# Decode rows of the token-major projections: fp32 on four column groups of TensorE instead of a fifth tile of split products

## The chip, the cores and the metric

The kernel runs on one NeuronCore of a Trainium2 chip. The metric is the device time of one execution in microseconds; the median of several runs is compared. The profile is one execution taken by the hardware profiler. Engines are called PE (TensorE, the matrix engine), DVE (VectorE), ACT (ScalarE), POOL (GpSimd) and SP (SyncE, which issues the DMAs).

## The reference

One inference step of a decoder of two layers, for two groups of requests that share all weights: a prompt of 512 tokens, and eight sequences that decode one token each. Each layer normalises and modulates its input, projects it, runs three token mixers side by side (retention, differential attention, RWKV-7), merges them by gates, and ends with a squared-ReLU MLP. What the change touches is one line of it, for the columns of retention and of differential attention:

```
h = rms_norm(x, p['norm1'][l]) * (1 + sc1) + sh1
z = jnp.einsum('bld,de->ble', h, p['w_in'][l])
z_ret, z_diff, z_rwkv, z_gate = jnp.split(z, [...], axis=-1)
```

`h` has 1024 columns, `z_ret` 2048 and `z_diff` 1536. All is float32, for 512 + 8 tokens.

## The kernel before

Activations lie with the model dimension on the partitions: `hT` is 8 tiles (k) of 128 rows by T = 520 tokens, of which the last 8 are the decode tokens. A product in fp32 is made of three in the type fp32r: both operands are split in a high and a low part, and high x high, low x high and high x low are added up in PSUM. ACT makes the high part of a weight block (`split_hi`, L546), DVE the low part (`split_lo`, L554), each for half a block (four of the eight k tiles, 128x2048) at a time, into the two pairs of buffers `w_split`. PE's matrix products are all issued from L379 (`mm`) and its transposes from L382.

`token_major` (L803) makes the projections whose result has tokens on the partitions. It is called twice in each layer: for retention with four blocks of 512 columns (L921), and for differential attention with three (L1128). A block `b` has two halves `n = 2b` and `2b + 1` (`u` is 0 or 1), one for each half of the contraction. For each half PE goes over five tiles of tokens m: four of 128 prompt tokens, and a fifth that starts at token 512, has the 8 decode tokens in its first rows, and takes the next 120 columns of `h_raw` along. Each tile has one PSUM bank, `pb[m]`, and each half of it is 4 k tiles x 3 products of 128x128 (activations, held in the array) by 128x512 (weights, streamed):

```
for x, (h, w) in enumerate(((0, wh), (1, wh), (0, wl))):
    t = mm(pb[m], h_raw[h][:, tk], w[:, k, :], start=(u == 0 and k == 0 and x == 0),
           stop=(u == 1 and k == 3 and x == 2))
```

Behind the second half of a tile ACT copies the bank into `arena` (L872): 128x512, and 8x512 for the fifth. The order on ACT within a block is: wait for the end of the first half (`split_free`), split the first half of the next block, five evictions, split the second half of the next block.

The weights come by SP's `load_w` (L531) into two ring slots of 2 MB, block b into slot b % 2; the first two are loaded ahead, the loads of blocks 2 and 3 wait until DVE has split the last half of the block that holds the slot (`slot_free`). In the retention stage SP then issues the first loads of gate weights (`gate_load`, L746). At this stage's start (`before`) DVE and ACT make the activation tiles one by one (`h_ready` counts them) while PE already runs the first half, k by k.

Where PE multiplies nine conditioning rows by a weight block (`ada_rows`, L1191, and `rows` in `start_pe`), the kernel has a form of its own: fp32 without a split, the operand held in the array is 128x32, the k tiles go to four groups of 32 columns of the array in turn (output partitions 0, 32, 64 and 96), and a product with the constant `fold` adds the four partial sums.

All stages are separated by block barriers. The semaphores of the table `sems` are cleared one by one on POOL (`clear`, L372) before the layers and at the end of each.

Of the kernel before, what the change touches and what calls it, by code (L numbers as in the profile page):

```python
# [23 lines left out]
P = 128  # L24
D = 1024
KD = D // P
# [178 lines left out]
def build(nc, a, consts, outs):  # L205
# [7 lines left out]
    with ExitStack() as ctx:  # L213
# [29 lines left out]
        rstd = sb("rstd", T)[:, :]  # L243
        small = sb("small", 512)[:, :]
        pages = sb("pages", DEC * NPG, I32, 1)[:, :]
        AR = 18688
        arena_at = aligned(nc.sbuf_base)
        arena = sb("arena", AR)[:, :]
# [50 lines left out]
        def sem(name):  # L299
# [1 line left out]


        sems = {n: sem(n) for n in (
            "split_high", "split_ready", "split_free", "y_split", "slot0_full", "slot1_full", "slot2_full", "slot3_full", "slot0_free", "slot1_free", "slot2_free", "slot3_free", "loaded", "states_loaded", "stored",
            "pe_for_dve", "dve_for_pe", "pe_for_act", "act_for_pe", "dve_for_act", "act_for_dve",
            "dve_done", "act_done", "dve_for_sp", *(f"page{n}_full" for n in range(10)), "page_free",
            "scores_ready", "scores_read", "logits_ready", "exp_ready", "weights_ready", "turned", "turned_read",
# [33 lines left out]
        up_made, up_read, kk_scaled, kk_factor, kk_spread = sems["up_made"], sems["up_read"], sems["kk_scaled"], sems["kk_factor"], sems["kk_spread"]  # L341
        split_high, split_ready, split_free = sems["split_high"], sems["split_ready"], sems["split_free"]
        y_split_ready = sems["y_split"]
        loaded, stored = sems["loaded"], sems["stored"]
        states_loaded = sems["states_loaded"]
        dve_for_sp = sems["dve_for_sp"]
# [79 lines left out]
        with nc.Block() as block:  # L426
# [57 lines left out]
            @block.vector  # L484
            def _(v):
                dv = c["dve"]
                dv(V.memset(tab[NB:NB + 1, :], MASKED))
                dv(V.memset(small, 0.0))
                dv(V.memset(eps, EPS))
                dv(V.memset(eps_ln, LNX_EPS))  # L490
                for h in h_raw:
                    dv(V.memset(h.bitcast(F32)[:, KD * T:], 0.0))
                for k in range(KD):
                    v.wait_ge(pe_for_dve, c["dve_from_pe"].next())
                    V.tensor_copy(xT[:, k, 0:SEQ], pb[k % 4])
                    dv(V.tensor_copy(xT[:, k, SEQ:T], pb[4 + k % 4][:, 0:DEC]))
                    V.sem_inc(dve_for_pe, 1)
                v.wait_ge(act_for_dve, c["dve_from_act"].next())
                dv(V.tensor_tensor(c_gate, c_gate, c_rows, mult))
                V.sem_inc(dve_for_pe, 1)  # L500
                v.wait_ge(pe_for_dve, c["dve_from_pe"].next())
                dv(V.tensor_copy(csT.rearrange("p k s -> p (k s)"), pb[0][:, 0:72]))
                V.sem_inc(dve_for_pe, 1)
                v.wait_ge(pe_for_dve, c["dve_from_pe"].next())
                for h in range(HB):
                    V.tensor_copy(biases[:, h, 0:512], pb[h])
                    V.tensor_copy(biases[:, h, 512:640], pb[4 + h][:, 0:128])
                dv(V.tensor_copy(biasD.rearrange("p g h -> p (g h)"), pb[4][:, 256:256 + NPG * HB]))
                V.sem_inc(dve_for_sp, 1)
# [3 lines left out]
        with nc.Fori(0, DEPTH) as l:  # L513
# [164 lines left out]
            def start_v(v):  # L678
# [49 lines left out]
                for k in range(KD + 1):  # L728
                    if k < KD:
                        V.tensor_scalar(ht[:, k, 0:SEQ], ht[:, k, 0:SEQ], coef[:, k, 0:1],  # L730
                                        modT[:, k, 0:1], mult, add).then_inc(dve_for_act, 1)
                    if k:
                        v.wait_ge(act_for_dve, c["dve_from_act"].next())
                        V.tensor_tensor(hT[1][:, k - 1], ht[:, k - 1], hT[0][:, k - 1].bitcast(F32), sub).then_inc(h_ready, 1)
                dv(V.tensor_tensor(lam, small[:, 6:7], small[:, 7:8], sub))
                dv(V.tensor_tensor(lam, lam, li[:, bass.ds(l, 1), 0:1].rearrange("p a b -> p (a b)"), add))
                dv(V.tensor_scalar(BR("subln"), BR("subln"), li[:, bass.ds(l, 1), 1:2].rearrange("p a b -> p (a b)"), None, mult))
# [62 lines left out]

            upper = ((4, 5), (6, 7))

            def token_major(col0, n_blocks, n_split, gates=False, before=None):  # L803


                with nc.Block() as block:
                    @block.sync
                    def _(sp):
                        if before:
                            before[0](sp)  # L810
                        for b in range(2, n_blocks):
                            load_w(sp, b % 2, w_in[:, col0 + 512 * b:col0 + 512 * (b + 1)])
                        if before:
                            sp.wait_ge(h_ready, KD)
                        if gates:
                            for j in range(4):
                                gate_load(sp, j)

                    @block.tensor
                    def _(pe):  # L820
                        if before:
                            before[1](pe)
                        def product(u, m, k):
                            tk = slice((4 * u + k) * T + m * P, (4 * u + k) * T + (m + 1) * P)
                            wh, wl = (w_split[u][x].rearrange("p (k n) -> p k n", k=4) for x in range(2))
# [3 lines that stand above are left out]
                            return t  # L829

                        for n in range(2 * n_blocks):
                            u = n % 2
                            pe.wait_ge(split_ready, c["split_ready"].next())
                            if before and n == 0:

                                pe.wait_ge(act_for_pe, c["pe_from_act"].next(5))
                                for k in range(5):
                                    pe.wait_ge(h_ready, k + 1)
                                    for m in range(4 if k < 4 else 0):
                                        product(0, m, k)  # L840
                                    if k:
                                        t = product(0, 4, k - 1)
                            for m in (() if before and n == 0 else range(5)):
                                if u == 0:
                                    pe.wait_ge(act_for_pe, c["pe_from_act"].next())
                                for k in range(4):
                                    if before and n == 1 and m == 0:
                                        pe.wait_ge(h_ready, 5 + k)
                                    t = product(u, m, k)
                                if u:  # L850
                                    t.then_inc(pe_for_act, 1)
                            if u == 0:
                                t.then_inc(split_free, 1)
                        c["pe_from_act"].skip(5)

                    @block.scalar
                    def _(s):
                        S.sem_inc(act_for_pe, 5)
                        if before:
                            before[2](s)  # L860
                        if n_split == 0:
                            split_hi(s, w_split, 0, 0, 0)
                        split_hi(s, w_split, 1, 0, 1, first=False)
                        for b in range(n_blocks):

                            s.wait_ge(split_free, c["split_free"].next())
                            if b + 1 < n_blocks:
                                split_hi(s, w_split, 2 * b + 2, (b + 1) % 2, 0)
                            for m in range(5):
                                r = P if m < MT else DEC  # L870
                                s.wait_ge(pe_for_act, c["act_from_pe"].next())
                                c["act"](S.activation(arena[0:r, (b * 5 + m) * 512:(b * 5 + m + 1) * 512],  # L872
                                                      pb[m][0:r, :], ACT.Copy))
                                S.sem_inc(act_for_pe, 1)
                            if b + 1 < n_blocks:
                                split_hi(s, w_split, 2 * b + 3, (b + 1) % 2, 1, first=False)
                        if gates:
                            gate_hi(s, 0)
                            gate_hi(s, 1)
# [38 lines left out]
                return pe_part, dve_part  # L918


            token_major(RET0, 4, 1, gates=True, before=(start_sp, start_pe, start_s, start_v))  # L921
            Z = lambda b: at(arena, b * 2560, 5, 512)
            rot = [at(arena, 10240, 5, 512), at(arena, 12800, 5, 512)]
            qkT = at(arena, 0, 8, T)
# [200 lines left out]
                    pe_part(pe)  # L1125


            token_major(DIFF0, 3, 0)  # L1128
            w_ada_rest = L("w_ada")[:, 4 * 512:12 * 512]
            NA = 6  # L1130
            zq, zk, zv = Z(0), Z(1), Z(2)
# [1566 lines left out]
```

## Time and profile before

| | us |
|---|---|
| median of three runs | 3099.26 |
| lowest, highest | 3096.32, 3105.85 |
| span of the profiled execution | 3092.7 |
| PE busy in it | 2704.7 |
| DVE busy | 1464.7 |
| ACT busy | 820.6 |

The span runs from the first to the last instruction of the profiled execution; the runs' times hold also what lies around it. A line of the views in order of time has the start and the length in us, the engine, the line of the kernel, the operation, what it writes and reads with shapes, how many instructions are merged, and in brackets the idle time of the engine just before and what ended it. PE's records overlap: the distance of their starts tells the rate. One fp32 product leaves two records, one in fp32r leaves one.

### The profile page before, as it was taken

To read this page: it belongs to the slowest core of one execution; us is meant where nothing else is said; L and a number is where in the kernel's file an instruction comes from. 1 tells how busy PE (TensorE), PEld (TensorE's weight loads), DVE (VectorE), ACT (ScalarE), POOL (GpSimd) and SP (SyncE) were. 2 spreads that over 40 slices of the span, in tenths; PEclk is the share of its full clock that TensorE was granted. 3 is DMA by queue.
4 is the path that set the end of the run, shared out by engine and by line. 5 is a ranking of instruction groups with operands and counts; after the bars stand their busy time and mean duration, and the time that the engine had idled before them with its cause. 6 is when DMAs were issued, how large, how long until landed. Compare 5 with 4: busy or idle time off the path is not lost. (4 is left out here: it accounts for less than half of the span.)

```text
span 3092.7 us, 53427 instructions
## 1 busy us (share of the span) xinstructions
PE 2704.7 (87%) x22862; PEld 2389.3 (77%) x22862; DVE 1464.7 (47%) x2073; ACT 820.6 (27%) x1218; POOL 162.0 (5%) x102
## 2 busy tenths in 40 slices
PE   5988888997698898999969879888967979799997
PEld 3777775886588698999958768567946859799997
DVE  3344346434655665334351541744366566633443
ACT  1221214223311323333222111332241114333331
POOL 0011110300000000000000210112000000000000
PEclk9997999996599799999979879999956989899999
DMA  6222345721000341222341330656010015322232
GB/s 257 98 59 58 113 134 185 228 72 52 14 3 3 126 177 66 98 82 83 137 148 35 86 120 23 219 183 200 16 52 15 3 44 178 110 83 82 83 110 109
DMA packets 216310, 305.16 MB, mean 99 GB/s; under 512 B 28021, under 2 KB 97191, under 8 KB 214786
## 3 DMA queue, kind: packets, MB, share of 16 engines
q1 hardware_dynamic: 216066, 301.67, 29.0%
q8 instruction: 182, 2.98, 0.4%
q14 instruction: 62, 0.51, 0.1%
HBM read 266.49 MB, written 35.14 MB: 98 GB/s over the span
## 5 line engine op out<-in xcount | busy, mean ns | idle before, releaser
L379 PE MATMUL pb<-h_high,f_high 128*128 128x260 f32 x1984 | 401.5, 284 | 4.9 <-DVEq L2619 4.9
L379 PE MATMUL pb<-h_low,f_high 128*128 128x260 f32 x1984 | 398.6, 282 | 0.0
L379 PE MATMUL pb<-h_high,f_low 128*128 128x260 f32 x1920 | 387.7, 283 | 0.0
L554 DVE TENSOR_TENSOR w_low<-ring,w_high 128x2048 fp32r<-128x2048 f32 x66 | 151.3, 2293 | 405.7 <-ACT w_high L546 404.3
L379 PEld LDWEIGHTS pb<-h_high,f_high 128*128 128x128 f32 x1984 | 306.5, 188 | 5.3 <-issue 5.3
L379 PEld LDWEIGHTS pb<-h_low,f_high 128*128 128x128 f32 x1984 | 307.6, 189 | 0.0
L554 DVE TENSOR_TENSOR f_low<-ring,f_high 128x2048 fp32r<-128x2048 f32 x60 | 137.6, 2293 | 339.1 <-ACT h_high L548 214.2
L379 PEld LDWEIGHTS pb<-h_high,f_low 128*128 128x128 f32 x1920 | 294.5, 188 | 0.0
L757 POOL TENSOR_TENSOR g_low<-yT,g_high 128x512 fp32r<-128x512 f32 x96 | 159.9, 1670 | 1978.0 <-ACT g_high L753 1978.0
L379 PE MATMUL pb<-w_high,h_high 128*128 128x512 f32 x560 | 224.9, 402 | 20.9 <-DVEq L558 11.7
L379 PE MATMUL pb<-w_low,h_high 128*128 128x512 f32 x560 | 224.2, 400 | 0.0
L379 PE MATMUL pb<-w_high,h_low 128*128 128x512 f32 x560 | 224.0, 400 | 0.0
L546 ACT ACTIVATE w_high<-ring 128x2048 fp32r<-128x2048 f32 x66 | 126.2, 1917 | 333.2 <-PE pb L379 213.9
L546 ACT ACTIVATE f_high<-ring 128x2048 fp32r<-128x2048 f32 x62 | 118.8, 1916 | 352.9 <-PE pb L379 328.0
L379 PE MATMUL pb<-arena 64*64 64x64 f32 (+4 forms) x2320 | 188.4, 299 | 24.5 <-DVE arena L965 9.4
L379 PE MATMUL pb<-h_high,g_high 128*128 128x260 f32 x768 | 166.5, 300 | 42.9 <-POOL g_low L757 22.4
L379 PE MATMUL pb<-h_high,w_high 128*128 128x260 f32 x800 | 167.4, 292 | 31.7 <-DVE h_low L2513 17.1
L379 PEld LDWEIGHTS pb<-arena 64*64 64x64 f32 (+4 forms) x2320 | 141.6, 166 | 60.6 <-issue 40.5
L379 PEld LDWEIGHTS pb<-h_high,g_high 128*128 128x128 f32 x768 | 125.0, 199 | 60.6 <-POOL g_low L757 38.8
L379 PE MATMUL pb<-h_high,w_low 128*128 128x260 f32 x800 | 165.8, 290 | 0.0
L379 PE MATMUL pb<-h_low,w_high 128*128 128x260 f32 x800 | 165.2, 289 | 0.0
L379 PE MATMUL pb<-h_low,g_high 128*128 128x260 f32 x768 | 160.1, 291 | 0.0
(362 smaller groups left out, 4620.2 us busy)
## 6 DMA issues: line engine op xcount, KB each, us to landing
ring<-in_w_ff_dram SPq DMA_DIRECT2D x32, 2048.0 KB, 7.8
ring<-in_w_in_dram SPq DMA_DIRECT2D x20, 2048.0 KB, 9.1
ring<-in_w_ada_dram SPq DMA_DIRECT2D x18, 2048.0 KB, 8.1
yT<-in_w_in_dram SPq DMA_DIRECT2D x96, 256.0 KB, 3.6
arena<-in_w_ada_dram SPq DMA_DIRECT2D x9, 2048.0 KB
gate_spill_dram<-yT SPq DMA_DIRECT2D x48, 260.0 KB, 4.0
arena<-gate_spill_dram SPq DMA_DIRECT2D x12, 1040.0 KB, 5.4
arena<-in_cache_k_diff_dram SPq DMA_DIRECT2D x32, 256.0 KB, 3.1
```

The costliest lines, as they stand in the source:

```text
L379: return PE.matmul(out, lhsT, rhs, start=start, stop=stop, skip_group_check=True)
L546: t = S.activation(ws[n % 2][0], ring[slot][:, u * 2048:(u + 1) * 2048], ACT.Copy)
L554: t = V.tensor_tensor(ws[n % 2][1], ring[slot][:, u * 2048:(u + 1) * 2048], ws[n % 2][0].bitcast(F32), sub)
L757: G.tensor_tensor(g_split[j % 2][1], g_raw[j % 2], g_split[j % 2][0].bitcast(F32), sub).then_inc(gate_ready, 1)
```

## The change

The decode rows leave the five-tile scheme; the four prompt tiles stay. The eight columns of the activations are copied unsplit into a tile of their own, `dec_h` (8 k tiles of 32 columns, 24 of them zero), once a layer. Between the two halves of a block PE makes eight fp32 products, `dec_h[:, k]` (128x32) by the unsplit weights of the ring slot (128x512), k tile k on column group k % 4, into bank 4. ACT copies the bank to `dec_sum`; ahead of the third tile of the second half PE folds the four partial sums by one fp32 product with `fold` into bank 5, and ACT copies 8x512 of it to where the fifth tile's rows were put. Five semaphores are new. SP's loads into a ring slot wait also for the eight products that read it (`dec_made`). The scratch that is reserved for descriptors of dynamic DMAs is cut to 1024 bytes of a partition, which makes the room.

```diff
+        dec_h = sb("dec_h", KD * 32)[:, :].rearrange("p (k n) -> p k n", k=KD)
+        dec_sum = sb("dec_sum", 512)[:, :]
...
+                dv(V.memset(dec_h, 0.0))
...
+                    if k == 4:
+                        V.tensor_copy(dec_h[:, :, 0:DEC], ht[:, :, SEQ:T]).then_inc(dec_ready, 1)
...
                         for b in range(2, n_blocks):
+                            sp.wait_ge(dec_made, first_block + b - 1)
                             load_w(sp, b % 2, w_in[:, col0 + 512 * b:col0 + 512 * (b + 1)])
...
-                                pe.wait_ge(act_for_pe, c["pe_from_act"].next(5))
-                                for k in range(5):
+                                pe.wait_ge(act_for_pe, c["pe_from_act"].next(MT))
+                                for k in range(4):
                                     pe.wait_ge(h_ready, k + 1)
-                                    for m in range(4 if k < 4 else 0):
-                                        product(0, m, k)
-                                    if k:
-                                        t = product(0, 4, k - 1)
-                            for m in (() if before and n == 0 else range(5)):
+                                    for m in range(MT):
+                                        t = product(0, m, k)
+                            for m in (() if before and n == 0 else range(MT)):
                                 if u == 0:
                                     pe.wait_ge(act_for_pe, c["pe_from_act"].next())
+                                if u and m == 2:
+                                    pe.wait_ge(dec_copied, b + 1)
+                                    if b:
+                                        pe.wait_ge(dec_stored, b)
+                                    mm(pb[5][0:DEC, :], C("fold")[:, 0:DEC], dec_sum).then_inc(dec_folded, 1)
...
                             if u == 0:
                                 t.then_inc(split_free, 1)
-                        c["pe_from_act"].skip(5)
+                                pe.wait_ge(dec_ready, 1)
+                                if b:
+                                    pe.wait_ge(dec_copied, b)
+                                w = wslot(n // 2 % 2)
+                                for k in range(KD):
+                                    t = mm(pb[4][32 * (k % 4):32 * (k % 4) + 32, :], dec_h[:, k, :], w[:, k, :],
+                                           start=(k < 4), stop=(k >= 4))
+                                t.then_inc(dec_made, 1)
+                        c["pe_from_act"].skip(MT)
...
                                 split_hi(s, w_split, 2 * b + 2, (b + 1) % 2, 0)
-                            for m in range(5):
-                                r = P if m < MT else DEC
+                            s.wait_ge(dec_made, first_block + b + 1)
+                            if first_block + b:
+                                s.wait_ge(dec_folded, first_block + b)
+                            S.activation(dec_sum, pb[4], ACT.Copy).then_inc(dec_copied, 1)
+                            for m in range(MT):
+                                if m == 2:
+                                    s.wait_ge(dec_folded, first_block + b + 1)
+                                    S.activation(arena[0:DEC, (b * 5 + MT) * 512:(b * 5 + MT + 1) * 512], pb[5][0:DEC, :],
+                                                 ACT.Copy).then_inc(dec_stored, 1)
                                 s.wait_ge(pe_for_act, c["act_from_pe"].next())
...
+                        s.wait_ge(dec_stored, first_block + n_blocks)
...
-    nc = _bacc.Bacc("TRN2", target_bir_lowering=False, num_devices=1)
+    nc = _bacc.Bacc("TRN2", target_bir_lowering=False, num_devices=1, dynamic_dma_scratch_size=1024)
```

In the diff `b` on PE counts the blocks of both calls in a layer, since `first_block` is 0 for the first and 4 for the second.

## Rows read from the trace of the kernel before

**Rows 1.** Page, part 1: busy us (share of the span) xinstructions.

```profile
PE 2704.7 (87%) x22862; PEld 2389.3 (77%) x22862; DVE 1464.7 (47%) x2073; ACT 820.6 (27%) x1218; POOL 162.0 (5%) x102
```

**Rows 2.** Busy times by stretch: us from:to, length, engines, granted clock, DMA.

```profile
core 0: us, PE busy (x) PEld busy (x) DVE busy (x) ACT busy (x) POOL busy (x), PEclk, DMA share, GB/s
83.40:197.40 114.00, 114.00 (x480) 91.56 (x480) 23.53 (x23) 28.51 (x32) 0.00 (x0) 0.98 0.14 46
341.00:422.60 81.60, 81.58 (x351) 65.55 (x349) 9.17 (x4) 16.04 (x18) 0.00 (x0) 1.00 0.07 26
```

**Rows 3.** ACT in order of time, layer 0, retention: start us, us, instruction, idle.

```profile
127.61 1.92 ACT L546 ACTIVATE w_high<-ring 128x2048 fp32r<-128x2048 f32 x1 [11.43 <-PE pb L379]
...
130.40 0.60 ACT L872 ACTIVATE arena<-pb 128x512 f32<-128x512 f32 x1 [0.87 <-PE pb L379]
...
138.77 0.60 ACT L872 ACTIVATE arena<-pb 128x512 f32<-128x512 f32 x1 [2.20 <-PE pb L379]
...
141.55 0.59 ACT L872 ACTIVATE arena<-pb 8x512 f32<-8x512 f32 x1 [2.18 <-PE pb L379]
...
158.28 0.60 ACT L872 ACTIVATE arena<-pb 128x512 f32<-128x512 f32 x1 [0.87 <-PE pb L379]
```

**Rows 4.** PE in order of time, the same stage.

```profile
85.25 0.63 PE L379 MATMUL pb<-w_high,h_low 128*128 128x512 f32 x1
85.68 0.63 PE L379 MATMUL pb<-w_low,h_high 128*128 128x512 f32 x1
...
196.79 0.39 PE L379 MATMUL pb<-w_high,h_low 128*128 128x512 f32 x1
197.02 0.40 PE L379 MATMUL pb<-w_low,h_high 128*128 128x512 f32 x1
```

**Rows 5.** PE in order of time, differential attention, where `ada_rows` runs.

```profile
472.25 0.39 PE L379 MATMUL pb<-arena 128*128 128x128 f32 x2
472.57 1.93 PE L379 MATMUL pb<-ring,arena 128*32 128x512 f32 x16
474.42 0.49 PE L379 MATMUL pb<-arena 64*128 64x128 f32 x4
...
485.90 0.39 PE L379 MATMUL pb<-arena 128*128 128x128 f32 x2
486.12 0.96 PE L379 MATMUL pb<-cst,xT 128*128 128x9 f32 x8
```

**Rows 6.** Busy times by stretch, same stage; columns as in Rows 2.

```profile
482.70:484.60 1.90, 1.90 (x19) 0.45 (x18) 1.76 (x6) 0.28 (x1) 0.00 (x0) 1.00 0.00 0
487.00:490.00 3.00, 0.53 (x6) 0.34 (x5) 2.79 (x8) 1.62 (x5) 0.00 (x0) 1.00 1.03 398
491.30:494.40 3.10, 3.10 (x19) 0.62 (x18) 1.29 (x3) 0.28 (x1) 0.00 (x0) 0.59 0.18 65
```

**Rows 7.** PE in order of time, decode attention.

```profile
527.90 1.12 PE L379 MATMUL pb<-xT,cst 8*128 8x512 f32 x2 [1.15 <-DVEq L1384]
528.95 1.92 PE L379 MATMUL pb<-ring,arena 128*32 128x512 f32 x16
```

**Rows 8.** DVE, then PE in order of time, end of the last layer.

```profile
3070.30 0.17 DVE L2406 TENSOR_TENSOR xT<-xT,small 128x8 f32<-128x8 f32 x1
...
3079.88 1.53 PE L382 MATMUL pb<-cst,xT 128*128 128x128 f32 x6 [11.04 <-PEq L372]
```

**Rows 9.** DVE in order of time: set-up, and start of layer 0's retention stage.

```profile
15.79 0.69 DVE L495 COPY xT<-pb 128x512 f32<-128x512 f32 x1 [13.51 <-PE pb L382]
...
80.79 0.22 DVE L724 TENSOR_TENSOR yT<-yT,coef 128x64 f32<-128x64 f32 x1
```

**Rows 10.** SP's DMA issues in order of time, layer 0's retention stage.

```profile
76.66 42.57 SPq L531 DMA_DIRECT2D ring<-in_w_in_dram  x3
```

**Rows 11.** Page, part 6: weight loads, KB each, median us to landing.

```profile
ring<-in_w_in_dram SPq DMA_DIRECT2D x20, 2048.0 KB, 9.1
```

**Rows 12.** PE's first work behind layer 0's retention stage.

```profile
202.33 0.77 PE L379 MATMUL pb<-h_high,g_high 128*128 128x260 f32 x2 [4.91 <-PEq L806]
```

More of the change, by code:

```diff
@@ L303, in build @@
         sems = {n: sem(n) for n in (
-            "split_high", "split_ready", "split_free", "y_split", "slot0_full", "slot1_full", "slot2_full", "slot3_full", "slot0_free", "slot1_free", "slot2_free", "slot3_free", "loaded", "states_loaded", "stored",
+            "split_high", "split_ready", "split_free", "dec_ready", "dec_made", "dec_copied", "dec_folded", "dec_stored", "y_split", "slot0_full", "slot1_full", "slot2_full", "slot3_full", "slot0_free", "slot1_free", "slot2_free", "slot3_free", "loaded", "states_loaded", "stored",
             "pe_for_dve", "dve_for_pe", "pe_for_act", "act_for_pe", "dve_for_act", "act_for_dve",
@@ L343, in build @@
         y_split_ready = sems["y_split"]
+        dec_ready, dec_made, dec_copied = sems["dec_ready"], sems["dec_made"], sems["dec_copied"]
+        dec_folded, dec_stored = sems["dec_folded"], sems["dec_stored"]
         loaded, stored = sems["loaded"], sems["stored"]
@@ L801, in build, with token_major @@
             upper = ((4, 5), (6, 7))
-            def token_major(col0, n_blocks, n_split, gates=False, before=None):
+            def token_major(col0, n_blocks, n_split, first_block, gates=False, before=None):
                 with nc.Block() as block:
@@ L831, in _ @@
                         for n in range(2 * n_blocks):
-                            u = n % 2
+                            b, u = first_block + n // 2, n % 2
                             pe.wait_ge(split_ready, c["split_ready"].next())
                             if before and n == 0:
-                                pe.wait_ge(act_for_pe, c["pe_from_act"].next(5))
-                                for k in range(5):
+                                pe.wait_ge(act_for_pe, c["pe_from_act"].next(MT))
+                                for k in range(4):
                                     pe.wait_ge(h_ready, k + 1)
-                                    for m in range(4 if k < 4 else 0):
-                                        product(0, m, k)
-                                    if k:
-                                        t = product(0, 4, k - 1)
-                            for m in (() if before and n == 0 else range(5)):
+                                    for m in range(MT):
+                                        t = product(0, m, k)
+                            for m in (() if before and n == 0 else range(MT)):
                                 if u == 0:
                                     pe.wait_ge(act_for_pe, c["pe_from_act"].next())
+                                if u and m == 2:
[3 more added lines that the diff above has]
+                                    mm(pb[5][0:DEC, :], C("fold")[:, 0:DEC], dec_sum).then_inc(dec_folded, 1)
                                 for k in range(4):
@@ L853, in _ @@
                                 t.then_inc(split_free, 1)
-                        c["pe_from_act"].skip(5)
+                                pe.wait_ge(dec_ready, 1)
[7 more added lines that the diff above has]
+                        c["pe_from_act"].skip(MT)
                     @block.scalar
                     def _(s):
-                        S.sem_inc(act_for_pe, 5)
+                        S.sem_inc(act_for_pe, MT)
                         if before:
@@ L868, in _ @@
                                 split_hi(s, w_split, 2 * b + 2, (b + 1) % 2, 0)
-                            for m in range(5):
-                                r = P if m < MT else DEC
+                            s.wait_ge(dec_made, first_block + b + 1)
[7 more added lines that the diff above has]
+                                                 ACT.Copy).then_inc(dec_stored, 1)
                                 s.wait_ge(pe_for_act, c["act_from_pe"].next())
-                                c["act"](S.activation(arena[0:r, (b * 5 + m) * 512:(b * 5 + m + 1) * 512],
-                                                      pb[m][0:r, :], ACT.Copy))
+                                c["act"](S.activation(arena[:, (b * 5 + m) * 512:(b * 5 + m + 1) * 512], pb[m], ACT.Copy))
                                 S.sem_inc(act_for_pe, 1)
@@ L918, in heads_to_columns @@
                 return pe_part, dve_part
-            token_major(RET0, 4, 1, gates=True, before=(start_sp, start_pe, start_s, start_v))
+            token_major(RET0, 4, 1, 0, gates=True, before=(start_sp, start_pe, start_s, start_v))
             Z = lambda b: at(arena, b * 2560, 5, 512)
@@ L1125, in _ @@
                     pe_part(pe)
-            token_major(DIFF0, 3, 0)
+            token_major(DIFF0, 3, 0, 4)
             w_ada_rest = L("w_ada")[:, 4 * 512:12 * 512]
```

## The prediction

> **What bounds the kernel now.** I read the page's busy times first: PE works 87% of the span [rows 1], but that is an average over stages, and the change touches one kind of stage only, `token_major`. So the next view is the busy time of each engine in the stretches in which it runs: layer 0's retention stage (four blocks of 512 columns) from 83.4 to 197.4 us, its differential stage (three blocks) from 341.0 to 422.6, and the same two in layer 1, which read alike. PE is busy 114.00 of 114.00 us and 81.58 of 81.60; DVE has 23.53 and 9.17, ACT 28.51 and 16.04 [rows 2]. Nothing but PE can set the length. Then ACT's own order of time in one block: each eviction starts 2.79 us after the one before (138.77, 141.55), 0.60 long, with 2.18 to 2.20 us of idle that PE ends; the first evictions of two blocks stand 27.88 us apart (130.40, 158.28) [rows 3]. The eviction of 8x512 at 141.55 is the fifth, the decode tile: it holds 8 rows and waits as long as the others, because PE pushes 512 columns through for each product whatever the number of rows that count. Last, PE product by product: starts are 0.23 us apart (196.79, 197.02) and a record lasts 0.39 to 0.40; just after the stage's first start they are 0.43 apart (85.25, 85.68) [rows 4]. The granted clock of the four stretches is 0.98 to 1.00 [rows 2], so nearly all of it runs at 2.4 GHz, and the 0.43 belongs to the first 4 us of the stage, at 1.2 GHz.
>
> **The change, part by part.**
>
> Removed: in each block the fifth tile's 24 products, 12 in each half. By the evictions a tile's 12 take 2.79 us [rows 3], so 24 take 5.58 us of PE, all of it on the path. The fifth eviction (0.6 us of ACT) goes too, and is off the path except at the stage's end, where the fourth tile's eviction, as long, takes its place.
>
> Added on PE, first term: eight fp32 products of 128x32 by 128x512 on four column groups. The trace holds this very form, with the ring as moving operand, where `ada_rows` builds its modulation rows: 16 records (two per product) start at 472.57 and the next product starts at 474.42, 1.85 us later [rows 5]; the granted clock from 482.7 to 484.6, where another such group runs, is 1.00 [rows 6], and the three groups of that kind that I read at that clock agree within 0.01 us. Eight products one after another would be sixteen passes of 0.43 = 6.9 us, so the four groups do run side by side. I take 1.86.
>
> Second term: the fold, one fp32 product of 128x8 by 128x512. The nearest row is 8x128 by 8x512: two records at 527.90, the next product at 528.95, so 1.05 us [rows 7]. I take 1.05; it includes the passage to 32-column products behind it.
>
> Third term: the passage from the full-width stream into each of these two. A full-width product of 128 columns starts at 472.25 and the first 32-column one 0.32 later; the same product ahead of a full-width one takes 0.22 (485.90, 486.12) [rows 5]. So 0.10 for each passage, 0.20 in all.
>
> Sum for a block: 1.86 + 1.05 + 0.20 = 3.11 against 5.58, a gain of 2.47 us. There are 14 blocks (4 + 3 in each of two layers): 34.6 us.
>
> The Trainium skill speaks against the change here: TensorEngine Tiling (Array Packing), section Key Properties, says that a change of tiling mode drains TensorE. If each of four changes in a block cost what a record outlasts its spacing, 0.17 us, an estimate, the gain would be about 2.3 us a block and 33 in all; the rows at 472.25 show a passage of 0.10, so I keep the sum.
>
> Bounds of the unknown: at the least, four rounds of 0.43 (1.72) and two passes for the fold (0.86) with no passage at all: 2.58, gain 3.00, 42.0 in all. At the most, the longest record of such a group (1.92) and of the 527.90 product (1.12), and four passages of 0.40 - 0.23 = 0.17 each [rows 4]: 3.72, gain 1.86, 26.0 in all. I take the middle term by term because its rows are of the same form and clock.
>
> Semaphores: five more are cleared on POOL, by `clear`, three times (ahead of the layers and behind each). The end of the last layer shows the price: DVE's last addition ends at 3070.47, PE's next work starts at 3079.88 [rows 8], and between them lie the clears of the 117 semaphores in the table `sems`: at most 9.41/117 = 0.08 us each, 5 x 3 x 0.08 = 1.2 us, nothing hides it. Taken: 1.2; bounds 0 and 1.2.
>
> At nothing, with their cover: (a) DVE's copy of the eight columns into `dec_h`, 128x64, 0.22 us by its like at 80.79 [rows 9]. It stands in DVE's queue ahead of the fifth to eighth activation tile and the weight split behind them; PE wants these only when it has done 48 products, some 5 us later; without that cover it costs 0.22 a layer. (b) The clearing of `dec_h` at the start: DVE idles 13.51 us there until PE's first transposes [rows 9]. (c) ACT's copy of the partial sums, 0.6 us: ACT has just done the next block's split (1.92 us, 127.61 [rows 3]), the eight products end about when the split does, so the copy is done 3 us after the half ends; PE wants it only before the third tile of the second half, 1.86 + 5.58 = 7.4 us after the half ends. Queued behind ACT's wait for these products are the evictions of the block, the first of which PE allows 4.7 us after the half; so some 2 us are spare. (d) PE's waits for `dec_copied` and `dec_stored` of the block before are met some 20 us ahead. (e) SP's new wait for `dec_made` holds the loads of blocks 2 and 3 and, behind them, the first four gate loads, until the block two before has had its eight products. Now the loads go out from 76.66 on, the last of three by 119.23 [rows 10]. The load of block 2 would leave at about 98 instead of 94, lands in 9.1 us (median) [rows 11], and is wanted when the first half of block 1 is done, 23 us after it leaves. The gate loads move from 120 to about 126 and are wanted at the stage's end, now near 188.
>
> What follows the stage: PE starts the next one 4.91 us idle [rows 12], behind the last eviction, two gate splits and the block's barrier; all of this hangs on the stage's end and moves up with it, and none of it waits for a time of its own.
>
> **Sum.** 34.6 - 1.2 = 33.4 us. The profiled execution's span is 3092.7; the three runs have a median of 3099.26 and a lowest of 3096.32, so some 4 to 7 us lie around the span. Span 3092.7 - 33.4 = 3059.3; median 3099.3 - 33.4 = 3065.9 us.
>
> **The rivals.**
>
> The column groups run one after another in this place (slower). Then the eight products are 6.9 us instead of 1.86, a block costs 8.1 against 5.58, and 14 blocks lose 35 us and 1.2: 3136. It decides from 4.3 us for the eight products on (5.58 less fold and passages). Against it: the same form at 1.85 and 1.86 us [rows 5]; for it only that there the neighbours are short products, and here a saturated stream.
>
> The clock falls (no change, or slower). From 487.0 to 490.0 PE was busy 0.53 of 3.0 us, and the next group of 32-column products ran at a granted clock of 0.59 [rows 6]. If the 32-column products of this change were followed by 4 us at 1.2 GHz, as at the start of the stage, each fall would lose half of these, about 2 us: 14 falls take 28 back and leave 3094; a fall for the fold too would give 3122. Against it: here no idle lies in front, and from 482.7 to 484.6, in a stretch of busy PE, such products ran at 1.00.
>
> The change doesn't free what it says, because something else ends the block. ACT's work in a block is 3.84 of splits and 3.6 of evictions, with one copy more 7.4 against 25 us; DVE's 4.6. Late weights: a load would have to take over 23 us instead of 9.1 before PE waits. Then the gain would shrink towards nothing, 3090 to 3100. I give it little.
>
> The gain is given back in part behind the stages, where later stages meet DMAs or clock falls in another phase: some 10 us of scatter, 3078 to 3090.
>
> **How the numbers follow.** Forecast (gain 25 to 42): 0.83. Given back in part, still over 0.3%: 0.07. Clock falls once a block, or late weights, within 0.3%: 0.05. Groups in series or two clock falls, slower: 0.05. A measurement of this kernel tells about 0.3%, 9.3 us, from no change: faster is below 3090, slower above 3108.6. Faster 0.90, same 0.05, slower 0.05. Range: from the largest gain, 42.0 with no price for the clears, 3057, to the smallest, 26.0 - 1.2, 3074.5; the runs of the kernel before spread some 3 us below and 6 above their median, so 3055 to 3079.
>
> **What would show each step.** The first evictions of neighbouring blocks stand 25.4 us apart instead of 27.9; the retention stretch is 104 us instead of 114, the differential one 7.4 us shorter; PE stays fully busy in both at a clock of 0.98 to 1.00; the sixteen records of the eight products span 1.9 us from start to the next full-width start, the fold 1.05. ACT shows no idle that ends with the fold. The gap at the end is 9.8 us instead of 9.4. The prediction is wrong if PE shows idle inside a block, if the eight products take over 2.5 us, or if the stages agree and the rest of the span is longer.

## The result, and the profile after

| | before | after |
|---|---|---|
| median, us | 3097.91 | 3065.63 |
| lowest to highest | 3096.32 to 3105.85 | 3065.35 to 3065.99 |
| span of the profiled execution | 3092.7 | 3064.2 |
| PE busy | 2704.7 | 2667.6 |
| ACT busy | 820.6 | 828.2 |
| DVE busy | 1464.7 | 1465.1 |

The ratio is 0.9888, with a 95% interval of 0.9869 to 0.9908: 32 us less. The forecast was 3065.9.

The busy times by stretch, of after, that answer to [rows 2] (us from:to, length, engines, granted clock, DMA): the retention stage of layer 0 and the differential one.

```profile
core 0: us, PE busy (x) PEld busy (x) DVE busy (x) ACT busy (x) POOL busy (x), PEclk, DMA share, GB/s
83.70:188.60 104.90, 104.88 (x456) 75.58 (x456) 23.65 (x24) 30.77 (x36) 0.00 (x0) 0.97 0.15 50
327.00:405.00 78.00, 77.84 (x338) 56.21 (x339) 11.51 (x6) 17.75 (x21) 0.00 (x0) 0.97 0.08 28
```

PE still fills both (in the second, the 0.16 us that are missing lie nearly all ahead of the stage's first split product at 327.16), so it is still the one thing that sets their length; the first is 9 us shorter. ACT has two copies more in a block and one eviction less, and 74 us of idle left.

ACT in order of time, one block of the same stage, of after (it answers to [rows 3]; start us, us, instruction, idle):

```profile
123.39 1.92 ACT L551 ACTIVATE w_high<-ring 128x2048 fp32r<-128x2048 f32 x1 [8.51 <-PE pb L383]
125.28 0.60 ACT L891 ACTIVATE dec_sum<-pb 128x512 f32<-128x512 f32 x1
128.24 0.60 ACT L898 ACTIVATE arena<-pb 128x512 f32<-128x512 f32 x1 [2.36 <-PE pb L383]
131.03 0.60 ACT L898 ACTIVATE arena<-pb 128x512 f32<-128x512 f32 x1 [2.19 <-PE pb L383]
131.98 0.59 ACT L895 ACTIVATE arena<-pb 8x512 f32<-8x512 f32 x1 [0.36 <-PE pb L383]
134.97 0.60 ACT L898 ACTIVATE arena<-pb 128x512 f32<-128x512 f32 x1 [2.40 <-PE pb L383]
...
153.74 0.60 ACT L898 ACTIVATE arena<-pb 128x512 f32<-128x512 f32 x1 [2.36 <-PE pb L383]
```

The copy of the partial sums (125.28) has no idle in front: when ACT has made its split, the eight products are done. It ends 2.4 us ahead of the first eviction and 5 us ahead of the fold. The first evictions of two blocks stand 25.50 us apart (128.24, 153.74), where it was 27.88 [rows 3]; 25.4 was forecast.

PE in order of time around the eight products and around the fold, of after; it answers to [rows 4, 5, 7]:

```profile
97.45 0.40 PE L383 MATMUL pb<-w_low,h_high 128*128 128x512 f32 x1
97.78 1.92 PE L383 MATMUL pb<-ring,dec_h 128*32 128x512 f32 x16
99.63 0.50 PE L383 MATMUL pb<-w_high,h_high 128*128 128x512 f32 x1
99.97 0.39 PE L383 MATMUL pb<-w_high,h_low 128*128 128x512 f32 x1
...
105.08 0.40 PE L383 MATMUL pb<-w_low,h_high 128*128 128x512 f32 x1
105.41 1.02 PE L383 MATMUL pb<-dec_sum,cst 128*8 128x512 f32 x2
106.37 0.50 PE L383 MATMUL pb<-w_high,h_high 128*128 128x512 f32 x1
106.71 0.39 PE L383 MATMUL pb<-w_high,h_low 128*128 128x512 f32 x1
```

Starts of full-width products are 0.233 us apart in a stream. Here 0.33 lies ahead of the eight products, 1.85 from their start to the next full-width one, and 0.34 behind that; from 97.45 to 99.97 it is 2.52 instead of two distances, 0.47: the eight products cost 2.05 us. In the same way the fold costs 1.63 - 0.47 = 1.16. Together 3.21 against the 5.58 removed: 2.37 a block, 33.2 for 14. Worked out in the same way for each of the 14 blocks, in both profiles of after, the eight products cost 2.05 to 2.06 us and the fold 1.16 every time.

The end of the last layer, DVE and then PE, of after (to be read against [rows 8]):

```profile
3041.83 0.17 DVE L2432 TENSOR_TENSOR xT<-xT,small 128x8 f32<-128x8 f32 x1
...
3051.77 2.60 PE L386 MATMUL pb<-cst,xT 128*128 128x128 f32 x11 [11.40 <-PEq L376]
```

From the addition's end to PE it is 9.77 us instead of 9.41: five more semaphores take 0.36. All three profiles with 117 semaphores show 9.41; of the six with 122, five show 9.77 and one 9.86.

SP's DMA issues in the retention stage, of after (to be read against [rows 10]):

```profile
76.96 48.84 SPq L536 DMA_DIRECT2D ring<-in_w_in_dram  x3
126.41 76.59 SPq L753 DMA_DIRECT2D yT<-in_w_in_dram  x5
```

The last weight load leaves by 125.80, 6.6 us later than before, and the gate loads behind it at 126.41. Nothing waits for either: PE has no gap in the stretch.

**Where the time went.** I cut each trace at the starts of the first and of the last split product of the four stages that the change touches; the rest is all else. The last column is a stretch inside the stages: how long, from each stage's first product on, the products still start 0.43 us apart, summed over the four. A microsecond there makes 1/0.427 products instead of 1/0.2326 and so loses 0.455.

| profile, us | retention 0 | differential 0 | retention 1 | differential 1 | the four | the rest | at 1.2 GHz |
|---|---|---|---|---|---|---|---|
| before | 113.62 | 85.09 | 113.71 | 86.10 | 398.5 | 2694.2 | 16.8 |
| before, second profile | 114.41 | 85.19 | 113.59 | 85.83 | 399.0 | 2697.0 | 18.1 |
| after | 104.61 | 78.63 | 104.07 | 78.06 | 365.4 | 2698.8 | 18.1 |
| after, second profile | 104.43 | 78.89 | 104.01 | 77.78 | 365.1 | 2705.5 | 17.7 |
| no fifth tile | 91.84 | 69.80 | 92.08 | 69.80 | 323.5 | 2703.1 | 23.2 |
| no fold | 99.88 | 75.77 | 99.50 | 75.27 | 350.4 | 2700.5 | 21.1 |
| one group | 124.48 | 94.57 | 124.50 | 94.10 | 437.7 | 2700.2 | 19.4 |
| two groups | 110.64 | 83.22 | 110.98 | 84.01 | 388.9 | 2707.2 | 16.0 |
| wide fold | 102.78 | 78.58 | 103.03 | 78.30 | 362.7 | 2700.7 | 20.2 |
| split fold | 101.94 | 77.08 | 101.24 | 77.16 | 357.4 | 2707.5 | 22.4 |

The four stages lose 33.1 us between the first profiles. The rest grows by 4.6, 1.1 of it the semaphores; whether the change made the other 3.5 is what the first experiment asks. The prediction had named just this, stages that agree and a longer rest, as a sign of being wrong.

### The profile page after: what moved, and what is told of

Read it like the earlier page. It is cut to its first block and busy times, and to the rows that moved or that the text cites. A ratio compares the mean times of both kernels' runs of the same rounds, so it can differ in the third digit from the quotient of the medians.

```text
span 3064.2 us, 53317 instructions
## 1 busy us (share of the span) xinstructions
PE 2667.6 (87%) x22778; PEld 2327.9 (76%) x22778; DVE 1465.1 (48%) x2076; ACT 828.2 (27%) x1232; POOL 167.4 (5%) x102
## 5 line engine op out<-in xcount | busy, mean ns | idle before, releaser
L383 PE MATMUL pb<-w_high,h_high 128*128 128x512 f32 x448 | 183.9, 410 | 21.7 <-DVEq L563 11.6
L383 PE MATMUL pb<-w_low,h_high 128*128 128x512 f32 x448 | 180.0, 402 | 0.0
L383 PE MATMUL pb<-w_high,h_low 128*128 128x512 f32 x448 | 179.9, 402 | 0.0
```

Source lines behind the costliest of these rows:

```text
L383: return PE.matmul(out, lhsT, rhs, start=start, stop=stop, skip_group_check=True)
```

## The experiments

**The two kernels again.** No edit; each is profiled a second time.

> The kernel before, unchanged, profiled a second time. In the traces of before and after the stages that the change touches are shorter by about 33 us, but the spans differ by 28.5 only: some 5 us are given back where decode attention starts (500 to 560 us). Theory 1 (scatter): the first profile of before was a quick one there; this one takes its ring and cache waits otherwise, and its span is 3092 to 3100 with the difference in the stages that the change does not touch. Theory 2 (given back by the change): this profile agrees with the first within 1 us at every stage border, and the 5 us are a cost of the change.

> The changed kernel, unaltered, on the chip of the three variants beside it, so that they are compared with it there, and profiled a second time. Theory (the change is worth what PE saves in its stages, the rest is scatter): ratio to before 0.989, 3062 to 3068; the four stages together 365 us from first to last product as in its first profile, give or take 2 us for the length of the slow-clock start of each stage, while the stages between them differ by some us from the first profile.

Measured: before again 3097.8, its span 3096.0 against 3092.7. After again 3072.3 (3069.8 to 3073.2) beside 3104.3 for before on that chip, ratio 0.9903 (0.9873 to 0.9934); its span 3070.6 against 3064.2. The 3072.3 lie outside the 3062 to 3068 expected: on that chip the kernel before is slower by 6.4 us too, and the gain is 32.0 us, as good as that of the first comparison. The four stages repeat within 0.5 us. The rest doesn't: it is 2694.2 and 2697.0 for the same kernel before, 2698.8 and 2705.5 for the same kernel after. The second profile of before falls behind the first by 9.7 us up to the start of decode attention, mostly from 440 us on, and wins some 6 back by the end. The largest single step is at the start of decode attention. DVE in order of time there, first of before, then of its second profile:

```profile
541.51 1.22 DVE L1393 TENSOR_TENSOR xT<-arena,pb 128x1024 f32<-128x1024 f32 x1 [6.05 <-DMA arena<-in_cache_k_diff_dram]
```

```profile
551.24 1.22 DVE L1393 TENSOR_TENSOR xT<-arena,pb 128x1024 f32<-128x1024 f32 x1 [9.29 <-DMA arena<-in_cache_k_diff_dram]
```

The second product with a page of keys waits 6.05 us for its page in one execution and 9.29 in the other, and starts 9.7 us later. In the second profile of after it is layer 1's decode attention that comes later, by 7 us, and layer 0's agrees within some 1 us. Ahead of the eight such products of a layer DVE stands idle for 37.4 us in layer 0 and 40.6 in layer 1 in the first profile of before, and for 42.1 and 42.1 in the second; of after for 42.1 and 37.3, then 42.1 and 42.1. So either kernel has long and short waits here, and the first profile of before was a quick one. Theory 2 falls: the same kernel starts layer 1's retention stage 6.0 us later in its second profile.

Theory 1 holds in this, that scatter of such a size is shown. That nothing at all is given back is not shown. The rest is 2694.2 and 2697.0 in the two profiles of before, and 2698.8 or more in all eight of other kernels, among them the one without the fifth tile, which has no new semaphores. The medians leave little room for it: 32.3 and 32.0 us less, where the four stages of the first profiles and the clears make 33.1 - 1.1 = 32.0. Why the pages land so differently was not tried.

**The fifth tile alone.** The kernel before, four tiles instead of five.

```diff
-                                    if k:
-                                        t = product(0, 4, k - 1)
...
-                            for m in (() if before and n == 0 else range(5)):
+                            for m in (() if before and n == 0 else range(MT)):
...
-                            for m in range(5):
+                            for m in range(MT):
                                 r = P if m < MT else DEC
```

> The kernel before without the fifth tile: its 24 products a block and its eviction are left out, so the projections of the eight decode rows are not computed; nothing is put in their place, and memory and loads stay as they were. Theory (PE's products set the length of a block): 14 x 24 x 0.2326 = 78.1 us less than before, about 3020, blocks 22.4 us apart instead of 28.0; with as much given back behind the stages as in the trace of the change, 3020 to 3027. Rival (the gain of the change comes from its other edits: the memory that moved, the loads held back): at most some us of gain, 3090 or more. Rival (another engine ends the block soon after PE gets shorter): blocks 24 us apart or more, with ACT or DVE not idle.

Measured: 3025.7 (3022.5 to 3028.4) beside 3096.4 for before, ratio 0.9766 (0.9749 to 0.9782): 70.6 us less. ACT's first evictions of two blocks, in order of time:

```profile
100.13 0.60 ACT L870 ACTIVATE arena<-pb 128x512 f32<-128x512 f32 x1 [0.87 <-PE pb L379]
...
122.54 0.60 ACT L870 ACTIVATE arena<-pb 128x512 f32<-128x512 f32 x1 [0.88 <-PE pb L379]
```

They are 22.41 apart, and PE ends the idle before each: nothing else steps in. The four stages are 75.0 us shorter. In this execution they ran 6.4 us longer at 1.2 GHz than in the first profile of before, which takes 2.9: 77.9 without that, and 78.1 was expected. With 78 us gone PE is still what bounds these stages, and neither the moved memory nor the held loads of the change are in this kernel: both rivals fall. What the moved memory and the held loads cost by themselves was not tried. The median fell by 70.6, some 4 us less than the stages; the rest is 2703.1 here, and why is open.

**One column group, and two.** All eight products on one group, or on two; fold and copy over as many partitions. Here for two:

```diff
-  mm(pb[5][0:DEC, :], C("fold")[:, 0:DEC], dec_sum).then_inc(dec_folded, 1)
+  mm(pb[5][0:DEC, :], C("fold")[0:64, 0:DEC], dec_sum[0:64]).then_inc(dec_folded, 1)
...
-  t = mm(pb[4][32 * (k % 4):32 * (k % 4) + 32, :], dec_h[:, k, :], w[:, k, :],
-         start=(k < 4), stop=(k >= 4))
+  t = mm(pb[4][32 * (k % 2):32 * (k % 2) + 32, :], dec_h[:, k, :], w[:, k, :],
+         start=(k < 2), stop=(k >= 6))
...
-  S.activation(dec_sum, pb[4], ACT.Copy).then_inc(dec_copied, 1)
+  S.activation(dec_sum[0:64], pb[4][0:64], ACT.Copy).then_inc(dec_copied, 1)
```

> The changed kernel with all eight products on the first column group, added up in place; the fold and the copy ahead of it go over 32 partitions instead of 128. Same products, same loads, same waits. Theory (four groups run side by side, and a round of two passes costs 0.43 whether one product is in it or four): 16 passes x 0.427 = 6.8 us instead of 1.7, 5.1 a block, 71.7 in all: 3137, slower than the kernel before by some 40 us. Rival (the eight products cost what they cost by their number and their passages, side by side or not): 3066, no change.

> The changed kernel with the eight products on two column groups instead of four, fold and copy over 64 partitions. Theory (rounds of two passes at 0.427 each set the price): eight rounds of one product pair instead of four, 1.71 us a block more, 23.9 in all: about 3089.5, still a little faster than before. Rival (four groups bring no more than two): as the changed kernel.

Measured: one group 3143.8 (3134.6 to 3154.2) beside 3096.4 for before, ratio 1.0156 (1.0124 to 1.0188); two groups 3097.1 (3089.8 to 3100.7) beside 3104.3, ratio 0.9976 (0.9959 to 0.9993), and 24.8 above the changed kernel on the same chip. The eight products in PE's order of time, first on one group, then on two:

```profile
97.27 7.05 PE L383 MATMUL pb<-ring,dec_h 128*32 128x512 f32 x16
104.25 0.50 PE L383 MATMUL pb<-w_high,h_high 128*128 128x512 f32 x1
```

```profile
96.64 3.63 PE L383 MATMUL pb<-ring,dec_h 128*32 128x512 f32 x16
100.20 0.50 PE L383 MATMUL pb<-w_high,h_high 128*128 128x512 f32 x1
```

From their start to the next product: 6.98 us on one group, 3.56 on two, 1.85 on four. That is 16, 8 and 4 passes of 0.427, one behind the other, and a remainder of 0.14 to 0.15 that stays. The four stages are 72.3 us longer than after with one group (71.7 without the difference at 1.2 GHz; 71.7 expected) and 23.5 with two (24.4; 23.9 expected). That the groups run side by side is the whole gain: on one group the same change is a loss, on two it is worth a quarter of a per cent. With one group the loss is 47 us by the medians, where some 40 was expected; the stages make 39 of it and the clears 1. The other 7 are not accounted for; this kernel's four runs lie 20 us apart.

**No fold.** The product with the constant and the eviction behind it are left out.

```diff
-                                if u and m == 2:
-                                    pe.wait_ge(dec_copied, b + 1)
...
-                                    mm(pb[5][0:DEC, :], C("fold")[:, 0:DEC], dec_sum).then_inc(dec_folded, 1)
```

> The changed kernel without the fold: the product with the constant and the eviction of its 8x512 are left out, so the decode rows' partial sums are never added up. By the trace of after the fold takes 1.16 us a block, its passages included (two full-width products are 1.63 us apart instead of 0.47). Theory: 14 x 1.16 = 16.3 us less than the changed kernel, 3049.3. Rival (the fold hides behind something, or its passages are paid anyway at the next wait): 0 to 8 us less.

Measured: 3053.2 (3044.6 to 3054.6) beside 3096.4 for before, ratio 0.9851 (0.9830 to 0.9872). That is 3.9 above the 3049.3 expected; the changed kernel was not run beside it, so no median tells what this is worth. The four stages are 15.0 us shorter than after; they had 3.0 us more at 1.2 GHz, 1.4 us: 16.3 without that, as expected. The fold is on the path with all of its 1.16 us.

**A fold of full width.** The constant is widened to 128 columns with zeros, in a tile of its own.

```diff
+        fold_w = sb("fold_w", P)[:, :]
...
-  mm(pb[5][0:DEC, :], C("fold")[:, 0:DEC], dec_sum).then_inc(dec_folded, 1)
+  mm(pb[5], fold_w, dec_sum).then_inc(dec_folded, 1)
```

> The changed kernel with the constant of the fold widened from 8 to 128 columns, the rest zeros, so that the fold is a full-width fp32 product and the array's column tiling does not change around it; its 8 rows are copied as before. Theory A (the 0.10 us lost on each side of the fold comes from going to 32-column products and back): the fold costs 0.86 instead of 1.16, 4.2 us less than the changed kernel in all. Theory B (it comes from going between fp32r and fp32, or from the product's own waits): no change within 1 us.

Measured: 3068.6 (3065.1 to 3069.6) beside 3072.3 (3069.8 to 3073.2) for the changed kernel on the same chip. PE in order of time around the fold:

```profile
104.43 0.39 PE L384 MATMUL pb<-w_low,h_high 128*128 128x512 f32 x1
104.66 1.02 PE L384 MATMUL pb<-dec_sum,fold_w 128*128 128x512 f32 x2
105.12 0.79 PE L384 MATMUL pb<-w_high,h_high 128*128 128x512 f32 x1
105.75 0.40 PE L384 MATMUL pb<-w_high,h_low 128*128 128x512 f32 x1
```

From the last product ahead of the fold (104.43) to the second behind it (105.75) it is 1.32 instead of two distances, 0.47, so the fold costs 0.86 (0.85 to 0.86 in all 14 blocks): two passes of 0.43, and nothing at its edges. It is still fp32 between fp32r products, with the same waits, so theory B falls: the 0.30 us belong to the 8-column form. By the rows of after, 0.10 of them lie ahead of the fold, 0.10 between it and the next product (0.96 instead of 0.86), and 0.11 behind that. In the four stages it makes 2.7 us, or 3.7 without the difference at 1.2 GHz, against 4.2 expected.

**The fold as a split product.** ACT's copy becomes the high part, DVE makes the low part from the same bank, and two fp32r products of full width add up.

```diff
+        dec_low = sb("dec_low", 512, F32R)[:, :]
+        fold_r = sb("fold_r", P, F32R)[:, :]
...
-                                    pe.wait_ge(dec_copied, b + 1)
+                                    pe.wait_ge(dec_split, b + 1)
...
-                                    mm(pb[5][0:DEC, :], C("fold")[:, 0:DEC], dec_sum).then_inc(dec_folded, 1)
+                                    mm(pb[5], fold_r, dec_sum, stop=False)
+                                    mm(pb[5], fold_r, dec_low, start=False).then_inc(dec_folded, 1)
...
+                    def dec_split_low(v, b):
+                        v.wait_ge(dec_copied, first_block + b + 1)
+                        V.tensor_tensor(dec_low, pb[4], dec_sum.bitcast(F32), sub).then_inc(dec_split, 1)
```

> A version that may beat both: the changed kernel with the fold done as the other products are, in fp32r on the full array. ACT's copy of the partial sums becomes the high part, DVE makes the low part from the same bank, and two products with a 128-column constant (fold, rest zeros) add up. Theory (the fold's price is PE time on the path, and DVE's extra 0.5 us lies beside it): two products at 0.2326 = 0.47 instead of 1.16, 0.69 a block, 9.7 us in all: 0.9968 of the changed kernel, about 3056, and 40 us under the kernel before. Rival (the longer chain, copy, then subtraction behind the next block's weight split on DVE, reaches PE late): PE idles ahead of the fold, no gain or a loss.

Measured: 3066.1 (3060.2 to 3067.2) beside 3072.3 for the changed kernel and 3104.3 for the kernel before on the same chip; ratio to before 0.9879 (0.9856 to 0.9903). PE around the fold, and DVE in the same block:

```profile
105.05 0.40 PE L385 MATMUL pb<-w_low,h_high 128*128 128x512 f32 x1
105.28 0.40 PE L385 MATMUL pb<-dec_sum,fold_r 128*128 128x512 f32 x1
105.52 0.39 PE L385 MATMUL pb<-dec_low,fold_r 128*128 128x512 f32 x1
105.75 0.39 PE L385 MATMUL pb<-w_high,h_high 128*128 128x512 f32 x1
```

```profile
99.80 2.29 DVE L563 TENSOR_TENSOR w_low<-ring,w_high 128x2048 fp32r<-128x2048 f32 x1 [5.55 <-ACT w_high L555]
102.24 0.69 DVE L914 TENSOR_TENSOR dec_low<-pb,dec_sum 128x512 fp32r<-128x512 f32 x1 [0.15 <-DVE w_low L563]
```

The fold is now two products among the others, 0.47 us, and the subtraction is done 2.4 us before PE wants it (no less in any of the 14 blocks), so the rival falls. The four stages lose 8.0 us against after, 9.9 without the 4.3 us more at 1.2 GHz; 9.7 was expected. Of this 6.2 us show in the medians. The 3056 expected was reckoned from the 3065.6 of the first comparison; on this chip the changed kernel itself takes 3072.3. It has the lowest median on this chip of the kernels that compute everything, and its runs don't overlap with those of the changed kernel beside it; they do with those of the wide fold.

## Why the prediction was right, point by point

**What bounds.** Right. Without the fifth tile the stages shrink by what its products took (77.9 us without the clock's part, 78.1 worked out), and PE fills the stages before and after.

**The eight products.** 1.86 was taken from `ada_rows`, and 1.85 stands there after. The passage into them, 0.10, is there too. What the sum left out is the passage back: the first full-width product behind them takes 0.34 to the next instead of 0.23, 0.11 more. In [rows 5] the product behind the group was a narrow one itself (64x128), so the row could not show it, and I counted one side of the passage only. This is the one term that was mis-sized: 0.10 a block, 1.4 us in all. The Trainium skill, TensorEngine Tiling (Array Packing), section Key Properties, says that a change of tiling mode drains TensorE; the trace agrees that it costs, 0.10 to 0.11 us at each of four changes in a block, less than the 0.17 that I had worked out for it. That a drain is what takes this time no run shows. My sum of 33 us there puts the 0.17 on two of the four changes only.

**The fold.** 1.05 + 0.10 = 1.15 was taken, 1.16 measured (0.10 ahead, 0.96 to the next product, 0.11 behind), and the kernel without it confirms 16.3 us.

**The sum of a block.** 3.11 was forecast and 3.21 measured; 2.47 gained against 2.37; 34.6 against 33.2 by PE's rows and 33.7 by the four stages without the difference at 1.2 GHz.

**The semaphores.** 0.40 each time was forecast; 0.36 at the end, and layer 0 starts 0.37 later than before. The clear between the layers was not read by itself.

**What was costed at nothing.** The copy into `dec_h` takes 0.19 on DVE and no product waits for it; loads and gate loads left later by what was worked out (126 for the gates, 126.41 measured) and nobody waits. One sign was told wrongly: ACT does show an idle that ends with the fold, 0.36 us at 131.98. It costs nothing, since the next eviction waits 2.40 us more for PE.

**The time around the span.** Wrong, but it enters the forecast of the span only. I took the 4 to 7 us between the span of before and its runs for what lies around a span. In the executions for which both are known it is 1.8 us (3065.99 and 3064.2; 3097.82 and 3096.0). The profiled execution of before was simply quicker than its runs. By its own span the forecast was 3059.3, and the profiled execution of after has 3064.2: 1.3 of the 4.9 us are the gain of 33.2 - 1.1 = 32.1 instead of 33.4, the others lie in the rest. That the median was hit within 0.3 us is luck: the forecast starts from 3099.3, where the comparison has 3097.9 for before, and the gain was 32.3 instead of 33.4; the two errors, 1.4 and 1.1, cancel. The gain itself was forecast to 1.1 us in the first comparison and to 1.4 in the second, 32.0.

**The rivals.** Groups one after another: the price was right (71.7 us worse than after on one group), the condition is not met. The clock: no split product runs 0.43 from the next except at the stages' starts, before and after. The granted clock of the two stages shown is 0.97 after, and 0.98 and 1.00 before [rows 2]. The 1.00 is a matter of the window: it opens at 341.0, but the stage's first product starts at 337.10 and its slow start lies between; from 337.0 to 422.4 the clock is 0.98. Another engine or late weights: not seen. Given back behind the stages: the first pair of profiles looks like it, and the second pair shows that the same kernels move by as much; that some of it is given back is not excluded, and the medians leave about 1 us for it.

## What to carry to other kernels

A few rows that ride along as a full tile cost what a full tile costs; find them as evictions of few rows with the same distance as the others, and price a replacement by a form that the kernel already has elsewhere, with the way in and the way out. Rows that need a quarter of the array's columns can be taken unsplit in fp32, and here nearly all of the gain hung on all four column groups working at once: 32 us with four, 7 with two, a loss with one. Here a small product that stands alone between full-width ones was cheaper written at full width too, 0.86 us instead of 1.16.

## What the hardware showed that was not expected

A change from full-width products to 32-column or 8-column ones and back cost 0.10 us on the way in and 0.11 on the way back, and 0.10 to 0.15 more lie between; fp32 between fp32r products at full width cost nothing beyond its two passes: 0.86 us for the fold, against 1.16.

At the start of each stage, after 4.1 to 5.9 us without a product, PE ran at 1.2 GHz for 2.7 to 6.1 us, differently in each execution of the same kernel; over four stages this sums to 16 to 23 us and moves the total by some 3 us. Why it differs stays open. It is as much as the edits of single experiments bring, so the stages were compared with this stretch taken out.
